# TensorE multiplies the ones matrix by itself while it waits, in a two-layer diffusion transformer in one kernel

## The reference

```python
def rmsnorm(t, w):
    tf = t.astype(F32)
    tf = tf * lax.rsqrt(jnp.mean(tf * tf, axis=-1, keepdims=True) + EPS)
    return (tf * w.astype(F32)).astype(t.dtype)

def conv_ffn(h, w_up, conv_w, conv_b, w_down):
    gate, val = jnp.split(dwconv_centred(h @ w_up, conv_w, conv_b), 2, axis=-1)
    return (jax.nn.silu(gate) * val) @ w_down

def reference(...):
    for i in range(DEPTH):
        sh1, sc1, g1, sh2, sc2, g2 = modulation(c, ada_w[i], ada_b[i])
        hl = rmsnorm(xl, norm_mix_w[i]) * (1 + sc1) + sh1
        ...
        xl = xl + g1 * yl
        xl = xl + g2 * conv_ffn(rmsnorm(xl, norm_ffn_w[i]) * (1 + sc2) + sh2,
                                ffn_w_up[i], ffn_conv_w[i], ffn_conv_b[i], ffn_w_down[i])
        ...
    return xl
```

## Time and profile before

| | |
|---|---|
| median of 3 runs | 3656.49 us |
| lowest and highest | 3654.77 and 3658.05 us |
| the profiled execution: its time | 3655.85 us |
| its span, first to last instruction | 3653.7 us |
| PE busy | 3303.3 us, 90% of the span |
| PE weight loads busy | 2787.3 us, 76% |
| DVE busy | 2391.6 us, 65% |
| ACT busy | 974.5 us, 27% |
| POOL busy | 1019.3 us, 28% |
| TensorE clock granted, mean share of 2.4 GHz | 0.960 |
| the four norms' stages begin at about | 0, 1062, 2021 and 2894 us |
| FFN 0 tail, FFN 1 tail | at 1989 to 2019 us, 3626 to 3650 us |

### The profile page before, as it was taken

How to read it: one execution, slowest core, us unless ns; L and a number is a source line. 1 busy time by engine, 2 the same in 40 slices (tenths; PEclk the granted TensorE clock), 3 DMA queues, 4 the chain that set the end, 5 groups by cost and what they waited for, 6 DMA issues and landing times. The chain is left out here.

```text
span 3653.7 us, 48736 instructions
## 1 busy us (share of the span) xinstructions
PE 3303.3 (90%) x17622; PEld 2787.3 (76%) x17622; DVE 2391.6 (65%) x2972; ACT 974.5 (27%) x1352; POOL 1019.3 (28%) x539
## 2 busy tenths in 40 slices
PE   5989988887889999999998668988898899999998
PEld 3889877776768888888887547777777678888886
DVE  7975099999645666666666436656664556666666
ACT  4111233333332111111111424444443221111111
POOL 1323155554222222222221131112111333333331
PEclk8999999999889999999999879999999999999999
DMA  5557210000411111111110200000002111111111
GB/s 203 184 190 262 79 47 1 0 0 16 141 41 41 35 40 40 36 38 34 35 45 0 78 8 10 5 5 5 5 2 81 47 50 42 52 52 46 46 46 58
DMA packets 64155, 196.38 MB, mean 54 GB/s; under 512 B 7665, under 2 KB 20849, under 8 KB 62641
## 3 DMA queue, kind: packets, MB, share of 16 engines
q1 hardware_dynamic: 47200, 164.36, 13.3%
q10 hardware_dynamic: 16848, 30.56, 2.4%
HBM read 176.02 MB, written 18.87 MB: 53 GB/s over the span
## 5 line engine op out<-in xcount | busy, mean ns | idle before, releaser
L1379 DVE SCALAR_TENSOR_TENSOR resid<-ps,mod,resid 128x512 f32<-128x512 f32 (+1 forms) x880 | 601.9, 697 | 472.3 <-PE ps L1275 472.0
L1282 PE MATMUL ps<-hf_hi,up_hi 128*128 128x512 f32 (+1 forms) x1760 | 652.9, 371 | 31.1 <-DVE hf_lo L283 22.1
L1282 PE MATMUL ps<-hf_lo,up_hi 128*128 128x512 f32 (+1 forms) x1760 | 652.0, 370 | 0.0
L1282 PE MATMUL ps<-hf_hi,up_lo 128*128 128x512 f32 (+1 forms) x1760 | 650.1, 369 | 0.0
L1250 POOL TENSOR_SCALAR up_hi<-up_raw 128x1024 fp32r<-128x1024 f32 x88 | 94.5, 1073 | 1160.8 <-PE ps L1282 1100.0
L1282 PEld LDWEIGHTS ps<-hf_hi,up_hi 128*128 128x128 f32 x1760 | 334.7, 190 | 88.3 <-issue 34.2
L1282 PEld LDWEIGHTS ps<-hf_hi,up_lo 128*128 128x128 f32 x1760 | 333.9, 190 | 56.4
L1282 PEld LDWEIGHTS ps<-hf_lo,up_hi 128*128 128x128 f32 x1760 | 334.8, 190 | 51.4
L1275 PE MATMUL ps<-act_hi,dn_hi 128*128 128x512 f32 (+1 forms) x880 | 332.9, 378 | 18.5 <-DVE act_lo L1400 16.1
L1331 ACT ACTIVATE conv<-ps,conv_w 128x1280 f32<-128x1280 f32 (+1 forms) x88 | 115.6, 1314 | 803.1 <-PE ps L1282 802.9
L1275 PE MATMUL ps<-act_lo,dn_hi 128*128 128x512 f32 (+1 forms) x880 | 326.6, 371 | 0.0
(11 more groups left out here) (237 smaller groups left out, 7009.7 us busy)
## 6 DMA issues: line engine op xcount, KB each, us to landing
up_raw<-in_up SPq DMA_DIRECT2D x88, 512.0 KB, 3.2
adaw_ring<-in_adaw SPq DMA_DIRECT2D x80, 512.0 KB, 4.0
dn_raw<-in_dn SPq DMA_DIRECT2D x44, 512.0 KB, 3.2
vr<-vr_out ACTq DMA_DIRECT2D x80, 128.0 KB, 3.4
adaw_first<-in_adaw SPq DMA_DIRECT2D x16, 512.0 KB, 22.0
wvr_raw<-in_wvr SPq DMA_DIRECT2D x8, 1024.0 KB, 6.8
x<-in_xT ACTq DMA_DIRECT2D x8, 640.0 KB, 16.7
r<-vr ACTq DMA_DIRECT2D x10, 512.0 KB, 3.8
```

The lines of the kernel that those rows point to most:

```text
L1282: mm = pe.matmul(c.psf[:, at:at + w], a[:, half, k, :], b[:, k, t:t + w], start=(k == 0 and a is up_hi and b is h_hi), stop=(k == KD - 1 a ...
L1379: dve.scalar_tensor_tensor(resid[:, m, t:t + w], c.ps[:, 6 + j % 2, 0:w], c.mod[:, gate + m, cond[t]:cond[t] + 1], resid[:, m, t:t + w], A ...
```

## The change

A helper `spin` makes PE multiply the 128x128 float32 ones matrix by itself `n` times and write the result to the first 128 columns of a bank that holds nothing in that place. No engine reads these results. `spin` is called, between waits for semaphores that the other engines raise anyway, in the norms (bank 4, all four calls), after the first tile of both FFNs (bank 7), in the tails of both FFNs (bank 1), and in the latents (bank 7). In the norm of MLA the single wait for `added` at 8 becomes eight waits with a spin after each. In the latents the single wait for `squared` at 4 becomes four waits with a spin ahead of each. No instruction of another engine changes.

```diff
+    def spin(self, pe, n, bank):
+
+        for i in range(n):
+            pe.matmul(self.ps[:, bank, 0:P], self.ones[:, :], self.ones[:, :], start=(i == 0), stop=(i == n - 1))
...
@@ normalise, PE @@
                 mm.then_inc(added, 1)
-            return
-        if summing:
-            pe.wait_ge(added, KD)
+        elif summing:
+            for k in range(KD):
+                pe.wait_ge(added, k + 1)
+                c.spin(pe, 5, 4)
         for t, m in groups:
-            mm = pe.matmul(c.psf[:, pad + t - first:pad + t - first + m], c.ones[:, :], total[:, t:t + m],
-                           start=True, stop=True)
-        mm.then_inc(summed, 1)
+            if x_in is None:
+                mm = pe.matmul(c.psf[:, pad + t - first:pad + t - first + m], c.ones[:, :], total[:, t:t + m],
+                               start=True, stop=True)
+        if x_in is None:
+            mm.then_inc(summed, 1)
+        c.spin(pe, 4, 4)
+        pe.wait_ge(logged, 1)
+        c.spin(pe, 4, 4)
+        pe.wait_ge(rstd_set, 1)
+        c.spin(pe, 5, 4)
+        pe.wait_ge(scaled, 1)
+        c.spin(pe, 6, 4)
+        pe.wait_ge(shifted, len(seqs))
+        c.spin(pe, 5, 4)
+        pe.wait_ge(hi_set, 1)
+        c.spin(pe, 5, 4)
@@ ffn, PE @@
             if not with_down:
-                return first_tile()
+                first_tile()
+                return c.spin(pe, 15, 7)
...
         tiles(pe, body)
+        pe.wait_ge(u_read, FT * 2 + 1)
+        c.spin(pe, 10, 1)
+        pe.wait_ge(u_read, FT * 2 + 2)
+        c.spin(pe, 5, 1)
+        pe.wait_ge(mult_set, FT)
+        c.spin(pe, 5, 1)
+        pe.wait_ge(hi_set, FT)
+        c.spin(pe, 5, 1)
         pe.wait_ge(lo_set, FT + 1)
@@ mla_latents, PE @@
-        pe.wait_ge(squared, 4)
+        for j in range(4):
+            c.spin(pe, 4, 7)
+            pe.wait_ge(squared, j + 1)
         total_of(A, c.ones, (0, 1))
         total_of(B, c.ones, (2,))
...
         mm.then_inc(folded, 1)
+        pe.wait_ge(rstd_set, 2)
+        c.spin(pe, 15, 7)
```

## The result

| | before | changed kernel |
|---|---|---|
| median | 3657.09 us (10 runs, 3654.71 to 3658.53) | 3665.22 us (10 runs, 3661.63 to 3672.38) |
| ratio, 95% interval | | 1.0024, 1.0014 to 1.0034 |
| the profiled execution: time, span | 3655.85, 3653.7 us | 3664.99, 3662.9 us |

The account below looks back on a forecast made before the run. PE was taken to run at half clock after idle waits, ten stretches totalling 46.79 us. Seven terms sum to -13.3 us, scaled to -12.9, so 3655.85 becomes 3643.0 us; range 3636 to 3652.

Parts of the forecast that it names:

- What one spin costs: Everywhere: a spin takes 0.234 us at the high clock, fits in PE's idle waits and delays nothing except in two places.
- First tiles: Behind both FFNs' first tiles: the clock holds and the half-speed stretches shrink by half, -1.75 and -2.53 us.
- FFN 0 tail: First four adds and first down product of FFN 0's tail run at the high clock: -1.8 us.
- MLA sum: MLA norm: line 300 takes 2.31 instead of 4.63 us, less five spins on the path (1.17): -1.15 us.
- MLA, after the sum: MLA norm: 29 spins fill the wait, so the projections' 4.54 us at half clock halve: -2.27 us.
- Latents: 16 spins beside ACT's squares start at the low clock and raise it; line 1540 shortens, less 0.4 delay: -2.3 us.
- FFN norms: Both FFN norms: nothing gained, since PE would then wait for DVE to finish block 1 of the input.
- GLA norm: GLA stage: nothing gained, since DVE is busy throughout; PE may start a microsecond or two late, hidden.
- rival 1: Every low-clock stretch pays half, FFN and GLA norms included, and the tails in full: 3634 us; chance 0.07.
- rival 2: Clock holds only behind first tiles and in tails, staying or falling low in norms and latents: 3648.3 or 3650 us; chance 0.15.
- rival 3: No gain reaches the end: other engines keep the waits, or the clock's rise moves elsewhere: 3652 to 3657 us; chance 0.08.
- rival 4: Slower: the clock does not count spins, so all run at 0.46 us: +25.2, 3681 us; chance 0.05.

Follow-up runs that it names:

- Experiment 2: Changed kernel with spin() emitting nothing, every added wait kept and the credits still behind them: 3677.25 us, 1.0059 against the kernel before.
- experiment 10: Kernel before plus one wait: in GLA, PE waits for hi_set before raising its credits; no spins: 3654.49 us, 0.9998.
- experiment 1: Changed kernel with PE's starting credits (signals telling POOL the split-weight buffers are free) raised before the norm's waits and spins: 3646.37 us, 0.9975 against before.
- experiment 7: As experiment 1, plus eight spins behind block 0 of each FFN's first tile: 3648.64 us, 0.9981 against the kernel before.
- experiment 3: As experiment 1, but without the spins in the norms' bank: 3646.18 us, 0.9976 against the kernel before.
- experiment 6: As experiment 1, without waits and spins in the FFN norms, and with GLA's left ahead of its credits: 3641.14 us, 0.9961 against before.
- experiment 5: Changed kernel with PE's waits and spins kept, but POOL raising the starting credits itself at the top of its part: 3650.33 us, 0.9988 against before.
- experiment 4: As experiment 1, but with spins in the norms alone: 3653.47 us, 0.9997 against the kernel before.
- experiment 9: As experiment 6, without the five spins behind the last MLA add, and two spins, not four, ahead of the latents' last square: 3640.37 us, 0.9961.
- experiment 11: As experiment 6, but with GLA's credits first: 3642.98 us, 0.9966 against the kernel before.
- experiment 8: As experiment 1, with the waits and spins ahead of the credits again in the two FFNs alone: 3654.44 us, 0.9997 against before.

## Why the prediction was wrong

**The view of the kernel now** was right: PE idle at the named places, half speed behind them, and an FFN loop in which a gain stays. Right as well was that a spin at the high clock costs 0.117 us a record: 30 records in 3.51 us behind the first tile. The row that I took it from was read wrongly, though: the 1.64 us and the 1.50 us ahead of line 842 are of the weight loads. PE itself was idle for 1.13 us there, so the row did not show a pause of PE of 1.50 us at the high clock.

**The step that failed** is in "What one spin costs": "no engine waits on them, and no other engine's list changes". No other list changes, but an engine did wait for what stands behind them. I had set the spins against the idle time of PE and asked which product comes next. The next things in PE's list were the credits, which no view of PE shows as work, because they take no time. That POOL waited 82.6 us for "PEq L389" before was in the trace, and I did not ask what stands at line 389. It was late without harm then; how much room it had was the question. Between POOL's last split and the first product there were 1.5 us of room in FFN 0 and 6.5 in MLA (2049.77 against 2043.29), and from the sum's start POOL's first split moved from 4.4 to 12.3 us in FFN 0 and from 0.2 to 10.0 in MLA. The splits then lengthened themselves, which I had not priced either, though the earlier trace rows show DVE at 3.67 and 1.48 us in one operation. I used this row to say that DVE sets the pace in the FFN norms and did not ask what makes it slow.

Point by point:

- First tiles: -1.50 for -1.75, and -2.53 for -2.53. Experiment 2, without spins, has -0.01 in FFN 0 and -0.79 in FFN 1.
- FFN 0 tail: -1.23 for -1.8. The adds were right to a hundredth (3.34 for 3.33 us). The 0.57 missing is the first down product, held up by spins that ran at 0.50, which I had priced at the high clock. It came later after `act_lo` than before (0.62 for 0.06 us), one of my signs of being wrong.
- FFN 1 tail: -1.77 for -1.5.
- MLA sum: +1.22 - 2.32 = -1.10 for -1.15.
- MLA, after the sum: forecast -2.27, measured +10.15 - 0.06. With the credits first the gain exists (-2.08), and two things I hadn't seen take it: +0.83 and +1.49.
- Latents: +0.49 - 2.99 = -2.50 for -2.3. The spins didn't begin at the low clock, as I had said: the clock fell just behind their start.
- FFN norms: forecast 0, measured +8.62 - 0.93 and +5.83 - 0.55: the credits. With the credits first the reasoning on DVE holds in FFN 0 (+0.20, +0.03, and a new wait of PE for DVE of 2.03 us, where I had said 2); in FFN 1 this new wait brought the clock down, +1.65.
- GLA norm: right in effect. PE's start came 4.11 us late, where I had said one or two, and experiment 10 shows no cost of such a delay.

The six places where spins alone decide were forecast at -11.0 and measured at -10.6. The rivals: 1 fell with the FFN norms, whose first tiles gained nothing at clock 1.00 (+0.03 in FFN 0 in experiment 1, -0.01 in FFN 1 in experiment 7), against the rule of the Trainium skill cited there (TensorE: Matmul & The Clock Gate, HAM oscillation). 2 fell, since the spins raised the clock in the latents and the MLA sum. 3 fell in experiment 3, where the spins' gains reach the end (0.9976). 4 named slower with the wrong mechanism; a spin never cost 0.46 us all along a stage. None named a signal that stands behind the added waits.

## What to carry to other kernels

When a wait is added to an engine's list, read the list onward to the next instruction that *signals*, not only to the next one that computes, and look up who waits for it and how much room it has; a wait "for the sequencer" of an engine is such a place. Filler work against a falling clock pays where the next real work is bound by TensorE (tails, first tiles, sums with ones: 0.2% in experiment 3, 0.4% in experiment 6) and brings nothing where another engine hands over block by block. If a transfer of work to an earlier or later time is free on its own engine, ask which engine it then runs beside.

## What the runs showed of the hardware

- The clock fell where PE had waited 2.24, 2.21 and 2.15 us, and in some kernels behind shorter waits. Behind about 2.04 us in FFN 0's first tile it fell in experiment 5 and held in experiments 1 and 4. Behind 1.96 us: MLA's second pair lost 1.5 us in the profiles of experiments 1, 6, 7, 9 and 11, and nothing in experiments 2, 3, 4, 5, 8 and 10, the changed kernel and the kernel before, where the same wait stands (1.96 us before, 1.98 in experiment 3 and in the changed kernel). What decides was not settled. The clock stayed at 1.00 behind 1.37 us (first tile) and the spins behind 1.40 us ran at full speed. A gap is not safe because it is shorter than the 4.3 us of the earlier trace rows.
- POOL's splits and DVE's two-input operations exclude each other, at 0.8 to 2.2 us for each meeting: 1.04 becomes 2.28 and 2.34 becomes 3.46 on POOL, 1.48 becomes 2.32 or 3.64 on DVE.
- The mean granted clock says little of the time: 0.968 in the slower kernel, 0.960 in the kernel before, 0.966 in experiment 4 with no gain, 0.965 in experiment 3 with 9 us of gain.
